# Mixture-of-experts weights: blocks of 64 rows on two 64-column lanes become blocks of 32 rows on four 32-column lanes

## What is computed

```python
flat_e = (g_idx * EXPERTS_PER_GROUP + e_local).reshape(-1)      # expert of each of the 2048 rows
...
hid = silu(ragged_dot(xs, w1, group_sizes)) * ragged_dot(xs, w3, group_sizes)   # (rows, 512)
ys = ragged_dot(hid, w2, group_sizes) * gate                                     # (rows, 1024)
```

## Time and profile before

| | |
|---|---|
| median of 3 runs | 3143.3 us (3139.86 to 3147.69) |
| the profiled execution: its own time | 3144.96 us |
| its span, first to last instruction | 3142.8 us |
| TensorE busy | 2948.4 us (94%) |
| VectorE, ScalarE, GpSimd busy | 1325.7, 989.1, 645.8 us |
| expert stage: first up product to end of the last | 2519.5 to 3075.7 us |
| mean granted TensorE clock | 0.97 |

### The profile page before, as it was taken

How to read it: one execution, slowest core, us unless ns; L and a number is a source line. 1 busy time by engine, 2 the same in 40 slices (tenths; PEclk the granted TensorE clock), 3 DMA queues, 4 the chain that set the end, 5 groups by cost and what they waited for, 6 DMA issues and landing times. The chain is left out here.

```text
span 3142.8 us, 41309 instructions
## 1 busy us (share of the span) xinstructions
PE 2948.4 (94%) x14448; PEld 1917.7 (61%) x14448; DVE 1325.7 (42%) x2003; ACT 989.1 (31%) x1530; POOL 645.8 (21%) x410
## 2 busy tenths in 40 slices
PE   8999999998999998999989999899999599999992
PEld 5666666546888887887448755699974233333330
DVE  4444444442111112144743555444453545555555
ACT  3333333201111112232133222233321155555553
POOL 1010000112433343443003421322230000000002
PEclk9999999999999999999989999999999789999996
DMA  2000000311111113225621000500021679998995
GB/s 102 21 21 28 21 21 14 135 40 55 40 53 53 41 67 114 93 94 220 244 113 53 1 34 27 203 14 14 28 105 67 255 266 412 411 412 324 412 410 195
DMA packets 113954, 411.16 MB, mean 131 GB/s; under 512 B 15890, under 2 KB 16850, under 8 KB 108962
## 3 DMA queue, kind: packets, MB, share of 16 engines
q1 hardware_dynamic: 99908, 375.57, 31.4%
q10 hardware_dynamic: 7952, 16.82, 1.5%
q0 software_dynamic: 5968, 17.13, 1.5%
HBM read 371.56 MB, written 42.00 MB: 132 GB/s over the span
## 5 line engine op out<-in xcount | busy, mean ns | idle before, releaser
L3044 PE MATMUL ps<-moe_ring,moe_xT 128*64 128x512 f32 x1536 | 345.1, 602 | 1.1 <-ACT moe_xT L3098 1.1
L99 PE MATMUL ps<-x1T_high,w_up_high 128*128 128x512 f32 x704 | 275.2, 391 | 3.5 <-PEq L3366 3.5
L99 PE MATMUL ps<-x1T_low,w_up_high 128*128 128x512 f32 x704 | 274.9, 391 | 0.0
L99 PE MATMUL ps<-x1T_high,w_up_low 128*128 128x512 f32 x704 | 274.8, 390 | 0.0
L3044 PEld LDWEIGHTS ps<-moe_ring,moe_xT 128*64 128x64 f32 x1536 | 107.1, 138 | 200.5 <-issue 188.2
L2948 DVE COPY moe_ring<-moe_raw_up 128x1024 f32 x240 | 160.9, 692 | 117.0 <-PE ps L3044 85.1
L454 DVE TENSOR_REDUCE top<-ps 128x1 f32<-128x256 f32 (+7 forms) x128 | 91.0, 753 | 241.0 <-PE ps L350 241.0
L3059 PE MATMUL ps<-moe_ring,moe_hidT 128*64 128x512 f32 x768 | 180.9, 603 | 5.8 <-ACT moe_ring L3092 4.0
L304 PE MATMUL ps<-x0T_high,qkv_high 128*128 128x512 f32 x384 | 162.8, 424 | 22.8 <-ACT v L549 10.0
L3092 ACT ACTIVATE moe_ring<-moe_raw_up 128x1024 f32 x144 | 152.1, 1057 | 98.6 <-PE ps L3044 67.0
L88 PE MATMUL ps<-xT,w_cols 128*128 128x512 f32 x384 | 168.8, 592 | 1.6 <-PEq L3443 1.6
(11 more groups left out here) (486 smaller groups left out, 5375.6 us busy)
## 6 DMA issues: line engine op xcount, KB each, us to landing
moe_raw_up<-in_w SPq DMA_DIRECT2D x256, 512.0 KB, 15.8
moe_raw_down<-in_w SPq DMA_DIRECT2D x128, 512.0 KB, 15.8
w_ada<-in_w_ada SPq DMA_DIRECT2D x48, 512.0 KB, 5.3
w_up<-in_ffn_w_up SPq DMA_DIRECT2D x22, 1024.0 KB, 4.8
w_down<-in_ffn_w_down SPq DMA_DIRECT2D x44, 512.0 KB, 3.5
y_rows<-moe_y ACTq DMA_DIRECT2D x96, 128.0 KB, 5.6
qkv_raw<-in_attn_w SPq DMA_DIRECT2D x22, 512.0 KB, 3.5
y_rows<-zero_rows SPq DMA_DIRECT2D x1, 8192.0 KB, 29.9
```

What stands on the lines that cost most here:

```text
L99: ins = pe.matmul(out, stationary, moving, start=start and n == 0, stop=stop and n == last)
L3044: ins = pe.matmul(ps[to, 2 + s, :], xT[:, n, rows], ring[:, up_slot(s, n), lane * DE:(lane + 1) * DE], start=n == 0, stop=n == UPS - 1)
```

## The change

`ROWS` becomes 32, and a step is four blocks ("quarters", `LANES` = 4) of one 128-row tile. With 32 rows a block needs 32 columns of the array, and four 32-column lanes run at once, each on 256 columns of the weight piece. Results of a quarter lie as 128 partitions x 256 columns (lane by lane), so silu, the multiply by the w3 part and the scaling of the output work on half as many columns, the hidden rows need two transposes, and one DMA with a rearranged address stores a quarter. Every quarter still copies all 12 pieces of its expert. The copies are dealt out anew: ScalarE 4 (up 1, 3, 5, down 1), VectorE 6 (up 0, 2, 4, 6, down 0, 2), GpSimd 2 (up 7, down 3). The owners of a step are read by `owners_of`, five to a step on each of the three copying engines. GpSimd's gather of the next step is issued behind up copy 7 of the second quarter. The table of owners, the step count and the row-number table of `stage_route` follow the new block size. `HALVES` is renamed `PIECES` throughout, and a constant of another stage, `ADA_HALVES`, `ADA_PIECES`.

The core of the diff:

```diff
@@ constants
-ROWS = 64
-HALVES = (TOP * T - EXPERTS) // ROWS + EXPERTS
-HALVES += HALVES % 2
-STEPS = HALVES // 2
-STEPS_MIN = EXPERTS // 2
+ROWS = 32
 COPIES = 8
+LANES = P // ROWS
+LANE = 2 * DE // LANES
+PIECES = (TOP * T - EXPERTS) // ROWS + EXPERTS
+PIECES += -PIECES % LANES
+STEPS = PIECES // LANES
+STEPS_MIN = TOP * T // P
...
@@ stage_route: the scale row, the table of owners, one spare column of row numbers
-            for h in range(NH):
-                sp.dma_start(m.gate2[h * ROWS:(h + 1) * ROWS, :],
-                             d["mod_row"][0, 5 * D + h * HALF:5 * D + (h + 1) * HALF].partition_broadcast(ROWS)
+            for lane in range(LANES):
+                sp.dma_start(m.gate2[lane * ROWS:(lane + 1) * ROWS, :],
+                             d["mod_row"][0, 5 * D + lane * LANE:5 * D + (lane + 1) * LANE].partition_broadcast(ROWS)
...
-            then(dve.tensor_scalar(last_f[:], end[:, EXPERTS - 1:EXPERTS], 0.5, 0.25 - 1.0, ALU.mult, ALU.add))
+            then(dve.tensor_scalar(last_f[:], end[:, EXPERTS - 1:EXPERTS], 1.0 / LANES, -1.0 / LANES - 0.5 + 0.5 / LANES, ALU.mult, ALU.add))
...
-            dve.tensor_copy(m.slot_token[:], token[:])
+            dve.memset(m.slot_token[:, STEPS:], T)
+            dve.tensor_copy(m.slot_token[:, 0:STEPS], token[:])
...
@@ stage_experts
-        hidT = sb("moe_hidT", [P, HT, ROWS])
-        y = [sb("moe_y0", [P, HALF]), sb("moe_y1", [P, HALF])]
+        hidT = sb("moe_hidT", [P, HT // 2, 2 * ROWS])
+        y = [sb("moe_y0", [P, LANE]), sb("moe_y1", [P, LANE])]
...
-        UP_BY = {"act": (1, 3, 5), "dve": (0, 2, 4, 6, 7)}
-        DOWN_BY = {"act": (0, 2), "dve": (1, 3)}
+        UP_BY = {"act": (1, 3, 5), "dve": (0, 2, 4, 6), "pool": (7,)}
+        DOWN_BY = {"act": (1,), "dve": (0, 2), "pool": (3,)}
...
-        low, high = slice(0, ROWS), slice(ROWS, P)
-        hid = hid_tile[high]
+        low, high = slice(0, P // 2), slice(P // 2, P)
+        lanes = [slice(lane * ROWS, (lane + 1) * ROWS) for lane in range(LANES)]
+        columns = [slice(lane * LANE, (lane + 1) * LANE) for lane in range(LANES)]
+        hid = hid_tile[high, 0:LANE]
+        STORED = 16
...
-            return (HT * s + n) % COPIES
+            return (HT * (s % 2) + n) % COPIES
         def down_slot(s, k):
-            return (HT * (1 - s) + k) % COPIES
+            return (HT * (1 - s % 2) + k) % COPIES
...
+        def owners_of(eng, i):
+
+            h = LANES * i
+            owners = {s: owner_of(eng, h + s) for s in range(LANES)}
+            if not isinstance(i, int):
+                owners[-1] = owner_of(eng, h - 1)
+            return owners
...
@@ GpSimd
-                if not isinstance(i, int):
-                    pool.wait_ge(x_turned, i)
-                    gather(i, i)
+                inner = not isinstance(i, int)
+                owners = owners_of(pool, i)
+                for s in range(LANES):
+                    h = LANES * i + s
+                    copy_up(pool, pool.tensor_copy, "pool", h, s, owners[s], range(UPS))
+                    if s == 1:
+                        pool.wait_ge(x_turned, i + 1)
+                        gather(i + 1, i + 1)
+                    if inner or s:
+                        copy_down(pool, pool.tensor_copy, "pool", h - 1, s - 1, owners[s - 1])
...
@@ TensorE: products, transposes, order of a step
-                    for lane, to in enumerate((low, high)):
-                        ins = pe.matmul(ps[to, 2 + s, :], xT[:, n, rows], ring[:, up_slot(s, n), lane * DE:(lane + 1) * DE],
+                    for to, cols in zip(lanes, columns):
+                        ins = pe.matmul(ps[to, 2 + s % 2, 0:LANE], xT[:, n, rows], ring[:, up_slot(s, n), cols],
                                         start=n == 0, stop=n == UPS - 1)
...
-                    for lane, to in enumerate((low, high)):
-                        ins = pe.matmul(ps[to, 4 + s, :], hidT[:, k, :],
-                                        ring[:, down_slot(s, k), lane * HALF:(lane + 1) * HALF],
+                    part = hidT[:, k % 2, k // 2 * ROWS:(k // 2 + 1) * ROWS]
+                    for to, cols in zip(lanes, columns):
+                        ins = pe.matmul(ps[to, 4 + s % 2, 0:LANE], part, ring[:, down_slot(s, k), cols],
                                         start=k == 0, stop=k == HT - 1)
...
-                for k in range(HT):
-                    ins = pe.transpose(ps[:, 6, k * ROWS:(k + 1) * ROWS], hid[:, k * P:(k + 1) * P], m.ident[high, high])
+                for k in range(HT // 2):
+                    ins = pe.transpose(ps[:, 6, k * 2 * ROWS:(k + 1) * 2 * ROWS], hid[:, k * P:(k + 1) * P],
+                                       m.ident[high, high])
...
-                h = 2 * i
+                h = LANES * i
+                inner = not isinstance(i, int)
                 turn_x(i)
-                if not isinstance(i, int):
-                    multiply_down(h - 2, 0)
+                if inner:
+                    multiply_down(h - 2, LANES - 2)
                     turn_hidden()
                 pe.wait_ge(x_out, i + 1)
-                multiply_up(h, 0)
-                if not isinstance(i, int):
-                    multiply_down(h - 1, 1)
-                else:
-                    pe.wait_ge(hid_done, 1)
-                turn_hidden()
-                multiply_up(h + 1, 1)
+                for s in range(LANES):
+                    multiply_up(h + s, s)
+                    if s == LANES - 1:
+                        break
+                    if inner or s:
+                        multiply_down(h + s - 1, s - 1)
+                    else:
+                        pe.wait_ge(hid_done, 1)
+                    turn_hidden()
...
@@ ScalarE
-                act.activation(hid, ps[low, 2 + s, :], ACT.Silu).then_inc(silued, 1)
+                act.activation(hid, ps[low, 2 + s % 2, 0:LANE], ACT.Silu).then_inc(silued, 1)
...
-                for lane, of in enumerate((low, high)):
-                    act.dma_start(d["y_rows"][ds(h * ROWS, ROWS), lane * HALF:(lane + 1) * HALF], y[s][of]
-                                  ).then_inc(stored[s], 16)
+                act.dma_start(d["y_rows"][ds(h * ROWS, ROWS), :].rearrange("r (l c) -> l r c", l=LANES), y[s % 2][:]
+                              ).then_inc(stored[s % 2], 16)
...
+                owners = owners_of(act, i)
+                for s in range(LANES):
+                    h = LANES * i + s
+                    copy_up(act, copy, "act", h, s, owners[s], range(HT))
+                    if inner or s:
+                        gate(h - 1, s - 1)
+                    if s == 0:
+                        turned_x(i)
+                    copy_up(act, copy, "act", h, s, owners[s], range(HT, UPS))
+                    if inner or s:
+                        turned_hidden(h - 1)
+                        if inner or s > 1:
+                            store(h - 2, s - 2)
+                        copy_down(act, copy, "act", h - 1, s - 1, owners[s - 1])
...
@@ VectorE
-                dve.tensor_tensor(hid, hid, ps[high, 2 + s, :], ALU.mult).then_inc(hid_done, 1)
+                dve.tensor_tensor(hid, hid, ps[high, 2 + s % 2, 0:LANE], ALU.mult).then_inc(hid_done, 1)
...
-                dve.tensor_tensor(y[s][:], ps[:, 4 + s, :], gate2[:], ALU.mult).then_inc(y_out, 1)
+                dve.wait_ge(stored[s % 2], STORED // 2 * (h - s % 2) + 16)
+                dve.tensor_tensor(y[s % 2][:], ps[:, 4 + s % 2, 0:LANE], gate2[:], ALU.mult).then_inc(y_out, 1)
...
+                owners = owners_of(dve, i)
+                for s in range(LANES):
+                    h = LANES * i + s
+                    copy_up(dve, dve.tensor_copy, "dve", h, s, owners[s], range(HT))
+                    if inner or s:
+                        gate(h - 1, s - 1)
+                    copy_up(dve, dve.tensor_copy, "dve", h, s, owners[s], range(HT, UPS))
+                    if inner or s > 1:
+                        copy_out(h - 2, s - 2)
+                    if inner or s:
+                        copy_down(dve, dve.tensor_copy, "dve", h - 1, s - 1, owners[s - 1])
             for s in range(2):
```

More of the change, by code:

```diff
@@ L1031, in on_scalar @@
                 turn_out(i)
[L1032 removed]
+            late = self.PER_LATE_HALF * (i - self.ADA_PIECES)
             if late >= 0:
@@ L2939, in wait_up_slot @@
                 earlier(eng, up_used, 8 * h + n - 3)
-            elif not (isinstance(h, int) and h < 2):
+            elif isinstance(h, int) and h < 2:
+                if h == 1:
+                    eng.wait_ge(up_used, n - 3)
+            else:
                 eng.wait_ge(down_used, 4 * h + n - 11)
@@ L3036, in multiply_up @@
             def multiply_up(h, s):
-                rows = slice(s * ROWS, (s + 1) * ROWS)
+                rows = lanes[s]
                 earlier(pe, hid_done, h - 1)
@@ L3121, in step @@
                 inner = not isinstance(i, int)
-                before = owner_of(act, h - 1) if inner else None
```

(29 more changed lines are left out.)

71 lines of the change are left out of this document (28 added, 43 removed).

## The result

The changed kernel takes 3209.4 us (3206.07 to 3213.32) against 3141.6 for the kernel before on the same chip: 1.0217 times as long, interval 1.0202 to 1.0232. The forecast was 3172, with 3220 as its upper end: the sign was right, the loss was 68 us where 29 were forecast.

A forecast was written before the change was run, and what follows sets the result against it. TensorE was taken to bound the expert stage, DMA close behind. 80 x 6.7 + 19 x 2.7 + 3 = 590 us against 556 is +34; end -5 gives +29, so 3172 us; 8-in-10 range 3112 to 3220.

The forecast's parts named there:

- rival 5: TensorE's sequencer: instructions and register waits for each piece add 0.9 us a quarter, 72 in all: 3244 us; chance 0.06.
- the end: End of the expert stage: shorter last down product, transposes, multiply and store issue, 5 us less (3 to 6).
- rival 3: GpSimd's copy takes 2.41 us and holds up VectorE: 3332 us; decides from 1.4 us a copy on; chance 0.05.
- the bound of 0.74: VectorE beside GpSimd: each GpSimd copy costs VectorE at most 1.05 - 0.15 - 0.16 = 0.74 us.
- the term 0.15: VectorE beside GpSimd: 0.15 us subtracted from GpSimd's 1.05 us copy to get its most cost to VectorE.
- TensorE's own work: TensorE alone in the expert stage: 80 x (3.5 + 1.75 + 0.2) + 20 x 1.1 = 458 us, 98 less.
- The fourth rival: TensorE's clock falls after the idle time at each of 19 step starts, costing 65 us: 3237 us; chance 0.06.
- if the clock isn't 1.00: Sign named ahead for TensorE: the forecast would be wrong if its clock isn't 1.00.
- The owner reads: ScalarE at a step's start: five reads make the first silu late, 2.7 us in each of 19 steps.
- Rival 1: The owner reads are hidden, so the expert stage takes 535 us and the kernel 3117, faster; chance 0.25.
- I take 6.7 us a quarter: ScalarE's queue in order ends about 0.05 us later than TensorE's 6.65 us round trip: 6.7 for each of 80 quarters.
- the DMA floor: DMA in the expert stage: 206 MB at 411 GB/s needs 501 us, which binds nothing at that rate.

The follow-up runs named there:

- the late reads: Changed kernel with each copying engine reading one owner at a step's start and the other four later in the step: 3187.0 us, 1.0155.
- before_lane_store: Kernel before the change, with a half's two store DMAs made one, the lane as its outermost dimension: 3311.0 us, 1.0539.
- the version with both edits: Changed kernel with four of five owner reads moved later in the step and silu ahead of up copy 3: 3180.9 us, 1.0134.
- half_loads: Changed kernel with only half of each up piece's columns loaded from the third expert on: 3197.6 us, 1.0177.

## Why the prediction was wrong in size

*Right.* The product (3.66 for 3.63), lanes at once, no cost of the sequencer (rival 5), the multiply's 0.42; from the last down piece to the next product 0.84 for 0.90; the end, -5.7 for -5. GpSimd's copy stayed below the 1.4 us from which rival 3 decides, and its price for VectorE is 0.47 us a copy, below the bound of 0.74 (in which no run shows the term 0.15) and far below the whole copy that a full block would cost. The estimate of 1.0 us for that copy, from the Trainium skill, GPSIMD Engine Reference, section 3.1, was low: the trace has 1.14 to 1.19 beside a busy VectorE.

*Wrong, but off the path.* TensorE's own work: 80 quarters at 3.5 + 1.75 + 0.2 were counted, and the down product, which the wait cuts in two, takes 1.48 + 0.64 = 2.12 us for 1.75, the transposes 0.33 for 0.2. That is 40 us over 80 quarters, and is why busy time fell by 58 and not by 100. The stores' saving of 1.6 MB is 2.1 (512 rows of 4 KB), which changes nothing.

*The clock.* The fourth rival, a clock that falls at every step's start, didn't come in that form: the typical interval into a new step is 9.54 us, and the late reads take 2.44 of it away. But a part of it came: the clock, 1.00 from 2600 to 2700, is 0.98 in the mean of the stage, and some 25 us at 1.2 GHz can have cost up to half of that, within the 17 us that are irregular. By its own sign ("if the clock isn't 1.00") this counts against the forecast.

*The owner reads.* 2.7 us a step forecast, 2.4 measured with the late reads, by the mechanism named: the reads stand between the down copy and the silu. Rival 1, the only one on the faster side, fell with it.

*The step that failed first: "I take 6.7 us a quarter".* It is ScalarE's queue added up in order, and it was sized too small. From the silu of this quarter to the next, the forecast has 2.67 us until the output's multiply is done, 0.65 until the store is out, and 3.38 for the down copy and two up copies: 6.70. The rows have 2.61, 0.74 and 3.77: 7.12. So the three copies with the gaps ahead of them are what was under-sized: 0.23, 0.19 and 0.15 us lie ahead of them, 0.57, where the sum left 0.2. The rows put the last two down to TensorE, but the up product had ended at 2847.80, 0.41 us before the copy ahead of the last gap did. So that slot was free, and the gap isn't a wait for it; what the trace has there are register and semaphore instructions of ScalarE's queue. The ring of silu, multiply, two copies, output multiply, store, down copy and two up copies has no slack, so each of these gaps is paid in full: 7.20, 7.15, 6.86 for 6.7, and 9.54 for 9.4. That makes 20 x (30.75 - 29.5) = 25 us. That the order matters is shown: with the silu one copy earlier, intervals of 5.91 and 5.97 appear. The next quarter, 6.87, has 2.62, 0.82 and 3.43, so the excess doesn't always lie in the same gap; how the 25 us divide over the gaps wasn't tried.

*The step that failed second: the DMA floor, 206 MB / 411 = 501 us, which "binds nothing".* It took the rate as a property of the bytes. The new store is one DMA whose outermost dimension is the four lanes, and its packets go to few of the 16 engines. An estimate from packet times, with four engines: 32 packets of 0.046 us are 1.47 us a quarter on each of them; with the 4 KB packets of the loads in between (0.159 each) a store takes 32 x 0.205 = 6.6 us and 0.9 packets are under way, as the traces have it (5.9, and about 1.0). A load is spread over all engines and lands with the slowest. So the floor is 348 loads x 8 x 0.159 + 79 x 1.47 = 559 us before the gathers, not 501. For the kernel before in that form, on two engines: 64 x (0.084 + 0.159) = 15.6 us for a store (14.7 in the trace), and 64 x 0.084 = 5.4 us a half, 443 + 48 x 5.4 = 702 of the 719 us of its stage.

The packets in the traces bear the four and the two out. Beside its data, each DMA has packets of 4 bytes: 16 for each store of the kernel before and for each load, 4 for each store of the changed kernel, 2 for each in `before_lane_store` (the store queue has 80 more that are there without these stores). The number of a store's packets under way at a time is above 4 for 61 of 96 us in the kernel before and for 1.7 of 309 us in the version with both edits; in `before_lane_store` it is above 2 for 1.9 of 414 us. And the lag of the few shows in the loads: from 2643.5 to 2650 in the changed kernel, where SyncE had nothing new to issue, only 3 to 4 of their packets are under way, as if the other 12 engines were done; such time adds up to 34 us between 2560 and 3060, against 1 us in the kernel before. Which engines carried a store no record shows. The effect of the form is shown from both sides (32 us less, 169 more), and packet size and GpSimd's copies are shown not to be it.

The Trainium skill, DMA: Bandwidth & Descriptors, section Why a DMA increments its semaphore by 16 and not by 1, says that a DMA is cut over the largest number of engines, up to 16, that divides the slowest dimension of both its sides; here four, and two. The traces agree (4 and 2 packets of 4 bytes a store, as above). I had counted the store's issues and bytes and not asked this of its shape.

In the changed kernel itself the loads cost 15 us of the 76 (`half_loads`), since the engines' order was slow enough to hide most of it. These 15 and the 25 above make 40 of the 42 us by which the stage's 632 passed the forecast's 590. But the slower DMA took away what the mending of that order would give: 99 us a stage by the intervals, 30 as measured, until the store was mended too.

## What to carry to other kernels

When units of work become shorter, add up every ring of waits through two engines' queues, not only the one through TensorE, and look for what is done once a step (here register reads) ahead of something due. When a store is rearranged, ask how many DMA engines its outermost dimension leaves it: loads that share them slow down while busy shares still look full. And where two limits lie 10% apart, mending the nearer one alone shows little; the rate at full DMA share tells whether the farther one has moved.

## What was not expected of the hardware

The same `rearrange` store gave 357 to 378 GB/s at a DMA share of 0.97 to 0.99 from ScalarE's queue, and 403 at 1.03 from GpSimd's. Why is open. There its packets are recorded as 4 KB, 32 to a store, with 16 packets of 4 bytes; yet in 36 of the 41 stores that stand apart from other DMAs of that queue between 2600 and 3050 at most 4 of the 32 are under way at a time. So each store may again lie on few engines, and not always on the same ones; which they are the trace doesn't say. GpSimd takes 0.75 us in the median to issue it; ScalarE takes 0.56 in the changed kernel, and 1.05 in the version with both edits, where loads are always waiting.

And the low rate doesn't show at once. The changed kernel, in two stretches that follow one another, and what SyncE waited for in the second:

```profile
2575.00:2625.00 50.00, 39.46 (x656) 21.78 (x648) 34.62 (x51) 31.45 (x40) 18.17 (x19) 1.00 1.03 411
2625.00:2675.00 50.00, 38.81 (x640) 21.13 (x628) 34.36 (x51) 32.17 (x41) 17.75 (x17) 1.00 0.89 335
...
SPq L2991 <- DVE moe_ring L2965: 9.1, 2, 8.6
SPq L3002 <- DVE moe_ring L2977: 5.8, 1, 5.8
```

With the same stores, the first has 411 GB/s. The second's 335 is for the most part want of a free place: SyncE waits 15 of the 50 us until a copy has freed one. Each load waits for the landing of the twelfth before it, so the other engines can run ahead of the few by 12 loads, some 15 us of work, before they stand still. The 6.5 us from 2643.5 on, in which 3 to 4 load packets are under way, are such a lag being made up; that 12 loads are its limit is argued from the order of the loads and wasn't tried. Whoever reads only a stretch like the first finds nothing wrong.
